# The side work of a three-layer sequence model: attention by a table of steps, the order of the products beside it, and a scan in eleven steps

## The reference, cut to what matters

```
def _hybrid_mixer(u, w_in, ...):
    proj = jnp.einsum('bsd,dp->bsp', u, w_in).astype(f32)
    (mq, mk, mv, mo, mi, mf, rq, rk, rv, rg, gq, gk, gv, gz, ga, gb) = jnp.split(proj, offsets, axis=-1)
    h_m = _mlstm(_heads(mq, M_HEADS), _heads(mk, M_HEADS), _heads(mv, M_HEADS), i_pre, f_pre)
    y_m = _head_rmsnorm(h_m, m_out_norm) * jax.nn.sigmoid(mo)
    h_r = _retention(_rope(_heads(rq, R_HEADS)), _rope(_heads(rk, R_HEADS)), _heads(rv, R_HEADS))
    y_r = _head_rmsnorm(h_r, r_out_norm) * jax.nn.silu(rg)
    qkv = jax.nn.silu(_causal_dwconv(jnp.concatenate([gq, gk, gv], axis=-1), g_conv))
    cq, ck, cv = jnp.split(qkv, 3, axis=-1)
    h_g = _gated_delta(_l2norm(_heads(cq, G_HEADS)), _l2norm(_heads(ck, G_HEADS)), _heads(cv, G_HEADS), ...)
    y_g = _head_rmsnorm(h_g, g_out_norm) * jax.nn.silu(gz)
    return jnp.einsum('bsm,md->bsd', jnp.concatenate([y_m, y_r, y_g], axis=-1).astype(u.dtype), w_out)
```

## Time and profile before

| | |
|---|---|
| median of three runs | 3654.03 us (3653.55 to 3658.63) |
| profiled execution | 3651.84 us, its span 3650.0 us, granted clock 0.967 |
| PE busy | 3389.2 us, 93% of the span |
| DVE, ACT busy | 1726.5 us (47%), 1334.7 us (37%) |
| attention, layer 0 | 436.0 to 625.2 us |
| delta rows, layer 0 | 625.2 to 709.4 us |
| attention and delta rows, layer 1 | 1628.0 to 1897.0 us |
| from the last Mamba products through LRU | 2893 to 3266 us |

### The profile page before, as it was taken

How to read it: one execution, slowest core, us unless ns; L and a number is a source line. 1 busy time by engine, 2 the same in 40 slices (tenths; PEclk the granted TensorE clock), 3 DMA queues, 4 the chain that set the end, 5 groups by cost and what they waited for, 6 DMA issues and landing times.

```text
span 3650.0 us, 38903 instructions
## 1 busy us (share of the span) xinstructions
PE 3389.2 (93%) x15366; PEld 2733.5 (75%) x15366; DVE 1726.5 (47%) x2415; ACT 1334.7 (37%) x1892; POOL 30.4 (1%) x62
## 2 busy tenths in 40 slices
PE   8999987799999999998878999998998988899998
PEld 6888755587888888876558788877777776678887
DVE  4443444655443444344465544455544556454433
ACT  4332334333332333233433333345444446433322
POOL 0000000000000000000000000000000000000000
PEclk9999999899999999999989999999999999999999
DMA  4333211103333233331110333321211222233232
GB/s 138 98 96 95 88 53 58 32 25 100 97 96 96 93 98 95 96 93 52 58 31 25 98 98 96 95 75 48 68 52 47 85 82 67 74 106 98 94 96 66
DMA packets 107396, 288.05 MB, mean 79 GB/s; under 512 B 22912, under 2 KB 34176, under 8 KB 107216
## 3 DMA queue, kind: packets, MB, share of 16 engines
q1 hardware_dynamic: 91696, 278.70, 24.6%
q10 hardware_dynamic: 14208, 2.63, 0.4%
q0 software_dynamic: 1312, 4.25, 0.4%
HBM read 282.64 MB, written 2.88 MB: 78 GB/s over the span
## 4 chain that ended last, share of the span: by engine, by line
PE 76%; DVE 11%; ACT 9%; issue 3%; DMA 1%; ACTq 0%; DVEq 0%; SPq 0%
PE ps L703 23%; PE ps L705 22%; PE ps L704 22%; DVE wl L1839 3%; ACT wh L1295 3%; DVE mf L2021 2%; PE ps L712 2%; PE ps L1024 1%; PE ps L1019 1%; DVE mf L2031 1%; PE ps L1190 1%; PE ps L717 1%; PE ps L1172 0%; PE ps L1186 0%; ACT mf L1427 0%
## 5 line engine op out<-in xcount | busy, mean ns | idle before, releaser
L1839 DVE TENSOR_TENSOR wl<-raw,wh 128x1024 fp32r<-128x1024 f32 (+3 forms) x581 | 651.8, 1123 | 1447.2 <-ACT wh L1295 1445.3
L703 PE MATMUL ps<-hnh,wh 128*128 128x512 f32 x2712 | 1098.6, 405 | 57.6 <-DVE mf L2516 29.0
L704 PE MATMUL ps<-hnl,wh 128*128 128x512 f32 x2712 | 1070.3, 395 | 0.0
L705 PE MATMUL ps<-hnh,wl 128*128 128x512 f32 x2712 | 1069.0, 394 | 0.0
L1295 ACT ACTIVATE wh<-raw 128x1024 fp32r<-128x1024 f32 (+3 forms) x581 | 567.1, 976 | 1046.7 <-PE ps L705 1027.9
L703 PEld LDWEIGHTS ps<-hnh,wh 128*128 128x128 f32 x2712 | 520.3, 192 | 201.2 <-issue 37.2
L705 PEld LDWEIGHTS ps<-hnh,wl 128*128 128x128 f32 x2712 | 517.7, 191 | 111.7
L704 PEld LDWEIGHTS ps<-hnl,wh 128*128 128x128 f32 x2712 | 519.5, 192 | 108.7 <-issue 4.3
L703 PE MATMUL ps<-mr,wh 128*128 128x512 f32 x1300 | 512.8, 394 | 16.4 <-DVE h L1965 9.3
L704 PE MATMUL ps<-mr,wh 128*128 128x512 f32 x1300 | 508.2, 391 | 0.0
L705 PE MATMUL ps<-mr,wl 128*128 128x512 f32 x1300 | 508.2, 391 | 0.0
(11 more groups left out here) (324 smaller groups left out, 2554.2 us busy)
## 6 DMA issues: line engine op xcount, KB each, us to landing
raw<-in_w_in SPq DMA_DIRECT2D x140, 512.0 KB, 3.5
raw<-in_ffn_w_gate SPq DMA_DIRECT2D x88, 512.0 KB, 3.5
raw<-in_ffn_w_up SPq DMA_DIRECT2D x88, 512.0 KB, 3.5
raw<-in_ffn_w_down SPq DMA_DIRECT2D x64, 512.0 KB, 3.5
raw<-in_w_ffn_in SPq DMA_DIRECT2D x44, 512.0 KB, 3.5
raw<-in_ffn_w_down SPq DMA_DIRECT2D x32, 384.0 KB, 3.1
raw<-in_w_out SPq DMA_DIRECT2D x32, 256.0 KB, 2.7
raw<-in_w_out_ssm SPq DMA_DIRECT2D x32, 256.0 KB, 2.6
```

What stands on the lines that cost most here:

```text
L703: self.e.matmul(out, ah, bh, start=start, stop=False, skip_group_check=shared)
L704: self.e.matmul(out, ah, bl, start=False, stop=False, skip_group_check=shared)
L705: m = self.e.matmul(out, al, bh, start=False, stop=stop, skip_group_check=shared)
L1839: self.e.tensor_tensor(lo[:, 0:n], k.raw[u % NRAW][:, 0:n], hi[:, 0:n].bitcast(F), ALU.subtract).then_inc(k.w_lo, 1)
```

## The change

**Attention.** The generator becomes a table of 65 steps. Step t does for head `t // 8` what its phase `t % 8` says, and beside it the norm of the pair before. All four scores of a head are issued at once into four banks (6, 7, 2, 3); spread and norm sums get a bank of their own (4). Rope starts at step 34, retention at step 40 with four steps a head. The four gated multiplies are put behind the table, since they need the gates, and the delta rows on ACT wait for the last of them. Zeroing and table loads on POOL start earlier.

**Order and pace.** The products beside the attention are now retention's q, k, v, the eight delta products, and gates 0 to 3 last. The paces rise.

**LRU.** The scan is cut into eleven steps, one operation for both channels each; the branch products 4 to 7 stand within the loop and behind it; gate product 8+i is followed by output product i at once. Of the rewritten functions only the new lines stand here.

```
 
-PACE_ROWS, PACE_ATT, PACE_DELTA = 0.9, 0.8, 1.0
-PACE_SSM_ROWS, PACE_SSM, PACE_LRU, PACE_LRU_GATES = 1.1, (1.1, 0.82, 0.82, 0.9), 0.25, 0.4
+PACE_ROWS, PACE_ATT, PACE_DELTA = 1.1, 0.98, 1.3
...
+ATT_STEPS, AT_ROPE, AT_RET = 65, 34, 40
+
...
         self.delta_qkv(l, 1)
-        self.qk_done = True
+        self.gates(l, y, 0, ACT.Sigmoid)
+        self.gates(l, y, 2, ACT.Silu)
         self.until(*self.work)
         self.pace = PACE_DELTA
         heads = [self.delta(l, h, y) for h in range(4)]
...
+        for t in range(ATT_STEPS):
+            h, s = divmod(t, 8)
+            p = h // 2 - 1
+            self.mlstm(l, h, s)
+            if 0 <= p < 2:
+                self.mlstm_pair(l, p, t - 16 * p - 16)
+            self.rope(l, t - AT_ROPE)
+            if t >= AT_RET:
+                h, s = divmod(t - AT_RET, 4)
+                self.retention(l, h, s)
+                for p in range(2):
+                    self.retention_pair(l, p, t - AT_RET - 8 * p)
+            yield
+        while len(self.gates_done) < 4:
+            yield
+        self.gated(l, y)
...
+        if s == 0:
+            self.wait_ge(k.row_v, 5 * l + 2)
+            self.wait_ge(*k.rows_v.at(l, "acol"))
+            if h:
+                self.wait_ge(*V.at(n - 1, "w3"))
+            if h == 3:
+                self.wait_ge(*k.mp_v.at(2 * l, "sum"))
+            self.spread(k.slot(M_NG, dt=R), h, B_PAIR, P.up(n, "sp"))
+            self.wait_ge(k.took, self.qk_took[2 * l])
+            for jt in range(4):
+                self.score(M_Q, M_K, h, jt, P.up(n, f"s{jt}"))
+        if s == 6:
+            self.wait_ge(k.took, self.v_took[2 * l])
+            if h:
+                self.wait_ge(*A.at(n - 1, "abs"))
+            for jt in range(2):
+                self.wait_ge(*V.at(n, f"w{jt}"))
+                self.values(M_V, M_D, h, jt)
+        if s == 7:
+            self.wait_ge(*V.at(n, "w2"))
+            self.values(M_V, M_D, h, 2)
+            self.wait_ge(*V.at(n, "w3"))
+            self.values(M_V, M_D, h, 3).then_inc(*P.up(n, "v"))
...
+        if s == 2:
             self.wait_ge(k.row_v, 5 * l + 1)
+            self.wait_ge(*k.mh_v.at(4 * l + min(2 * p + 2, 3), "dm"))
+            self.e.matmul(k.ps[B_PAIR][:, :], k.selr[0:64, 32 + 128 * p:160 + 128 * p], k.slot(M_EM, dt=R)[0:64, :],
+                          start=True, stop=True).then_inc(*k.mp_p.up(n, "pair"))
+        if s == 5:
+            self.wait_ge(*k.mp_a.at(n, "sq"))
+            self.e.matmul(k.ps[B_PAIR][:, :], k.c("bd64"), k.slot(M_Y + p)[:, :], start=True, stop=True).then_inc(*k.mp_p.up(n, "nm"))
...
+        if s == 0:
+            self.wait_ge(*(V.at(n - 1, "w3") if h else k.rope_v.at(4 * l + 3, "x")))
+            for jt in range(4):
+                self.score(R_Q, R_K, h, jt, P.up(n, f"s{jt}"))
+        if s == 3:
+            self.wait_ge(k.took, self.v_took[2 * l + 1])
+            self.wait_ge(*(A.at(n - 1, "num") if h else k.mh_a.at(4 * l + 3, "abs")))
+            for jt in range(4):
+                self.wait_ge(*V.at(n, f"w{jt}"))
+                m = self.values(R_V, R_D, h, jt)
+            m.then_inc(*P.up(n, "v"))
...
+        self.wait_ge(*k.att_v.at(l, "y3"))
...
+        if i < 2:
+            self.wait_ge(*self.k.mp_p.at(2 * l + i, "nm"))
         self.e.tensor_tensor(y[:, :], self.bank()[:, :], self.k.rs[:, :], ALU.mult).then_inc(self.k.took, 1)
 
...
+        for p in range(5):
+            u = [k.slot(L_U[p % 2] + i) for i in range(2)]
+            yl = [k.slot(L_YL[p % 2] + i) for i in range(2)]
+            for i in range(2):
+                self.product_h()
+                self.end_taps()
+                self.taps = self.lru_conv(p, i, u[i])
+            for i in range(2):
+                self.product_h()
+                self.take_yl(p, i, yl[i])
+                if i == 0:
                     self.end_taps()
+                    for j in range(2):
+                        self.split_u(p, j, u[j], uh[j])
+            if p in (1, 3):
+                self.branch_acc(4 + p // 2)
             self.finish()
+            self.lru_gates(p, uh)
+            self.uh_unit = self.u
+            self.work.append(self.scans(p, y))
+        self.pace = PACE_LRU_END
+        self.branch_acc(6)
+        self.branch_acc(7)
+        gate = [k.slot(n) for n in L_GATE]
+        parts = [k.pair(L_UH + i, L_LO[i]) for i in range(8)]
         for i in range(8):
+            self.product_h()
+            if i == 0:
+                self.gate_acc(7)
+            self.take_branch(8 + i, gate[i % 2], 8 + i)
+            self.finish()
             self.product(y, lambda j: (k.scan_a.at(j // 2, f"hi{j % 2}"), k.scan_v.at(j // 2, f"lo{j % 2}")))
+            self.take_mix(i, gate[i % 2], parts[i])
...
+        for t in range(SCAN_STEPS):
+            for i in range(2):
+                if t == 1:
+                    self.wait_ge(*V.at(p, f"la{i}"))
+                    e.activation(th[i][:, :], r[i][:, :], ACT.Tanh).then_inc(*A.up(p, f"tanh{i}"))
+                if t == 2:
+                    e.activation(r[i][:, :], r[i][:, :], ACT.Exp, scale=-1.0).then_inc(*A.up(p, f"a{i}"))
+                if t == 3:
+                    self.wait_ge(*A.at(p, f"a{i}"))
+                    e.activation(sq[i][:, :], r[i][:, :], ACT.Square).then_inc(*A.up(p, f"a2{i}"))
+                if t == 5:
+                    self.wait_ge(*V.at(p, f"t{i}"))
+                    e.activation(th[i][:, :], th[i][:, :], ACT.Sqrt).then_inc(*A.up(p, f"root{i}"))
+                if t == 9:
+                    self.wait_ge(*V.at(p, f"y{i}"))
+                    e.activation(y[2 * p + i][0][:, :], u[i][:, :], ACT.Copy).then_inc(*A.up(p, f"hi{i}"))
             yield
...
-            if h >= 2:
+            if h < 2:
+                e.wait_ge(*(k.mh_p.at(4 * l + 3, "sp"), k.mp_p.at(2 * l + 1, "pair"))[h])
+            else:
                 e.wait_ge(*k.rh_v.at(4 * l + h - 2, "w3"))
             e.dma_start(k.slot(R_TAB[h % 2])[:, :], k.I["ret"][h]).then_inc(k.loaded[f"ret{h % 2}"], 16)
-        e.wait_ge(*k.rp_v.at(2 * l + 1, "y"))
+            if h == 1:
+                e.wait_ge(*k.mh_p.at(4 * l + 3, "v"))
+                e.memset(k.slot(D_T1, dt=R)[:, :].bitcast(F), 0.0).then_inc(k.zeroed, 1)
+                e.memset(k.slot(D_T2, dt=R)[0:64, :].bitcast(F), 0.0).then_inc(k.zeroed, 1)
```

More of the change, by code:

```diff
@@ L485, in attention, with gated @@
     def attention(self, l, y):
-        yield
-        yield
-        yield from self.mlstm(l, y)
-        yield from self.rope(l)
-        yield from self.retention(l, y)
+        for t in range(ATT_STEPS):
[14 more added lines that the diff above has]
+        self.gated(l, y)
+    def gated(self, l, y):
+        pass
     def prepare(self, l, heads):
@@ new lines, in rope @@
+    def rope(self, l, s):
+        k = self.k
+        if s == 0:
+            self.wait_ge(k.loaded["rope"], 16 * (l + 1))
+            self.wait_ge(*k.mh_v.at(4 * l + 3, "w3"))
+        if 0 <= s < 2:
+            for n in (2 * s, 2 * s + 1):
+                self.wait_ge(k.took, self.qk_took[2 * l + 1] - 3 + n)
+                self.e.matmul(k.ps[B_SCORE[n]][:, :], k.slot(R_D, 3)[:, 0:128], k.slot((R_Q, R_Q + 1, R_K, R_K + 1)[n])[:, :],
+                              start=True, stop=True).then_inc(*k.rope_p.up(4 * l + n, "rot"))
@@ L1274, in scans @@
     def scans(self, p, y):
-        yield
-        yield
-        yield
+        for _ in range(SCAN_STEPS):
+            yield
     def take_mix(self, i, gate, parts):
```

522 lines of the change are left out of this document (188 added, 334 removed).

## The result

The changed kernel takes **3611.8 us** (3610.0 to 3612.0), against 3655.5 us for the kernel before beside it: a ratio of 0.9879, 95% interval 0.9864 to 0.9895. It is faster by 43.7 us. The forecast was 3584 us, a gain of 70; the range, 3532 to 3634, holds the result. So the direction was right and about four tenths of the gain did not arrive. The question is which of the three terms was too large, and whether something else took time.

What follows compares the result with a forecast made beforehand. PE was taken to bound the kernel, so only vanished PE waits save time. Attention 33, delta rows 24 and LRU 12 sum to 69 us, giving 3584 us; the 8-in-10 range was 3532 to 3634.

Steps and rivals of the forecast that it cites:

- slower case: Rival: each convolution product beside attention holds its ring plus half a head's DVE and ACT work; 3684 us, chance 0.05.
- looser ring: Rival: DVE and ACT overlap better than walked, LRU gains 45 and attention 45 us; 3540 us, chance 0.22.
- LRU term: LRU: gain of 12 us, from products that now cover waits beside the scans; bounds 0 and 50.
- attention term: Attention of both layers: old PE waits go, smaller ones come; gains 19 and 14, together 33 us.
- three new waits that were walked: Attention, PE waits: pair matmul 2.0 us, head 3's values 6, second pair's norm sum 3.5.
- the clock loss follows the waits: 9.5 falls to 3.5: Attention of layer 0: with 13 us of waits against 23, low-clock loss falls from 9.5 to 3.5 us.
- seams: Attention of layer 0: cost of changes between product and small matmul, 0.2 to 0.4 us each, falls from 15 to 13.
- I take 4.6 and 2.8 us: Delta rows: waits for the rows' sums and beta rows fall from 7.9 and 6.2 us, 6.7 gained.
- what the pace moves behind the products: Delta rows: pace 1.3 puts 6.8 us of products among inversion and round-trip waits, gaining 5 to 6 a layer.
- The walk of the period: LRU: following DVE's and ACT's work in order gives a period of 34.0 us, practically the old 34.1.
- the cover: LRU: two of four periods take a fifth product of 5.4 us, become only 2 us longer; 6.8 us gained.
- The rule on table loads: ACT: the skill's 2.66 us a switch, not 1.28, would make the summed gain 58 us instead of 69.

Runs made afterwards that it cites:

- e9: e2 with squares of q no longer waiting for the last gated multiply, and remainder 0.0 at the third layer: 3598.1 us.
- e4: e2 with the pace of the delta rows at 1.0 again instead of 1.3: 3607.6 us.
- e2: Changed kernel with the remainder in `due` set to 0.80 at the third layer and 0 where each mixer begins: 3600.9 us.
- e5: e2 with LRU's scan put back into large pieces at the old pace of 0.25, branches and gates in new places: 3617.1 us.
- e1: Changed kernel with the remainder in `due` set to 0.80 instead of 0.48 where the third layer begins: 3601.4 us.

## Why the prediction was right or wrong

**Direction and range: right, with errors that partly cancel.** The attention's waits for its own multiplies went, the LRU stalls shrank, and neither the slower case nor the looser ring came (no LRU period is under 32.7 us). But 9 us of loss in Mamba and 15 too few in the delta rows stand beside an LRU term that was too small, and inside the attention term two errors cancel, as told below. One sign that I had named for the slower case was badly chosen: convolution evictions more than 8 us apart beside mLSTM. They are, with a mean of 10.8 us from the first to the last of these two:

```profile
497.57 0.68 DVE L2024 TENSOR_TENSOR mf<-ps,mf 128x512 f32<-128x512 f32 x1
...
573.08 0.68 DVE L2024 TENSOR_TENSOR mf<-ps,mf 128x512 f32<-128x512 f32 x1
```

But no wait of PE on such an eviction is left in this stretch; PE's own small matmuls and its waits for values and norms fill the distance. The sign had to be a wait of a product for L2024, not a distance. It was already exceeded before, where the eight evictions beside retention stand 10.0 us apart in the mean; the 6.65 us of the earlier trace rows are the shortest distance, at the stretch's end:

```profile
559.52 0.68 DVE L2031 TENSOR_TENSOR mf<-ps,mf 128x512 f32<-128x512 f32 x1
...
629.57 0.68 DVE L2031 TENSOR_TENSOR mf<-ps,mf 128x512 f32<-128x512 f32 x1
```

**Attention, 33 us forecast, 25.3 measured.** The three new waits that were walked came in size (2.0, 6, 3.5 us against 2.2, 6.6, 3.6). For the longest the path was only half right. The list on ACT ran 10 us as walked, to 508.59, but the head's weights on DVE then stood behind a whole convolution round as well, split, low part, eviction, tap and taps, and PE had more work of its own than the one product assumed:

```profile
509.64 1.23 DVE L1830 TENSOR_TENSOR wl<-raw,wh 128x1024 fp32r<-128x1024 f32 x1 [5.70 <-ACT wh L1289]
...
513.71 1.15 DVE L2263 TENSOR_TENSOR mf<-ps,mf 128x512 f32<-128x512 f32 x2
```

```profile
514.54 3.32 PE L1029 MATMUL ps<-mf,mf 128*128 128x512 f32 x4 [6.58 <-DVE mf L2263]
```

Two terms failed. I gave rope and the first values 1.5 us, and the trace has 0.3, 3.7 and 1.6, that is 4 us more in layer 0. And "the clock loss follows the waits: 9.5 falls to 3.5" did not come true:

```profile
436.30:609.30 173.00, 154.16 (x635) 113.16 (x633) 84.55 (x136) 68.76 (x80) 3.60 (x8) 0.95 0.19 61
```

At clock 0.95 over 173 us the loss, counted as in the forecast, is 8.7 us, nearly as it was. Eight waits, up to 6.6 us long, left the share of the low level, 1.2 GHz, as it was with fourteen of up to 4.8 us.

A third term hides this in the total. For layer 0 I had 10 us from waits, 6 from the clock and 2 from seams. The named waits gave some 4 (23 to 18.6) and the clock 1, and still the stretch went from 189.2 to 173.0. PE's idle time fell by 4.7 us only, its busy time by 11.5 (165.7 to 154.2, with 7 matmuls less in the window, about 1.6 us). What fell with it are the changes between product and small matmul: from 34 to 24 in either direction, counted over the same products in both traces. So the seams, which were given 2 us, are the largest part of this gain, by what is left over; no run was made for them alone.

**Delta rows, 24 us forecast, 9.0 measured in the changed kernel.** Both steps failed in size, here for layer 0. The first, "I take 4.6 and 2.8 us": 6.9 and 3.1 came, a gain of 4.1 and not 6.7. Four gate products between the convolutions and the squares help little when the Silu of the last gate and its table load stand on ACT right before them; e9 shows 2 us of it to be the new wait. The second, that what the pace moves behind the products is taken off the inversion and the round trip: the inversion fell from 6.4 to 1.0, but PE then had less left to do behind the store, and the wait for the round trip rose from 6.7 to 9.2, so the two gave 2.9 us and not 5 to 6. Small waits grew by 1.9 us besides. At pace 1.0 (e4) the beta rows wait 6.2 us as before the change, so their 3.1 is the pace's doing and not that of the gate products. In all the pace gave 3.6 and 4.7 us where the text had 5 to 6. In layer 1 the remainder of `due` took 5 us of this again (154.6 in the changed kernel, 149.7 in e2).

**LRU, 12 us forecast, 15.7 measured.** The walk of the period was right: 34.0 against 34.1 us without the fifth product, 36 against 35.6 and 37.9 with it, and the cover 6.8 against 6.6. The other 9 us, where the last scans had been given 5.5, no run takes apart. The text read from the walk that the cut itself gains nothing; e5 shows that in the new loop 13.8 us go with the cut and its pace. The walk compared the new period with the old kernel's, not with what the new arrangement would cost uncut, 36 and 40 us.

**Mamba, 0 forecast, +9.0 measured.** The sentence "cuts elsewhere I take at 0" failed. I had treated the paces as local. They are not: the remainder is carried into every later part. It could have been worked out before the run from the number of calls, as above.

**The rule on table loads.** The sum stood by the row and not by the page, and the row held: after a load of 1.28 us the next operation begins 0.01 us later in the changed order too, as this row of e2 and its successor show.

```profile
605.87 1.28 ACT L1574 ACT_TABLE_LOAD   x1
607.16 0.69 ACT L1574 ACTIVATE mf<-ps,col 128x512 f32<-128x512 f32 x1
```

The Trainium skill ("ScalarE: Activation LUTs", What ACT_TABLE_LOAD costs) counts 1.38 us of draining on top; with it the list before head 3's values would have been 5.5 us longer. The trace does not agree: in the changed kernel that list, from its first load at 499.11 us to the end of the exponential at 508.59, takes 9.5 us with its four loads of 1.28 us and no gap above 0.02.

**The sum.** By stretches: 25.3 + 9.0 + 15.7 - 9.0 = 41.0 us, and the span fell by 40.2, the medians by 43.7. With the remainder of the third layer set as before (e1) the change is worth 50.6 us by the span and 55.9 by the medians.

## What to carry to other kernels

A pace with a running remainder couples every part to all later ones: reset it where a part begins, or a change of pace in one place retunes another, here by 9 to 10 us. When two engines alternate on one chain, compute the period by walking both lists in order; here the walk met the mean period with the cut, 34.0 against 34.1 us, but said nothing on what the uncut step would cost in the new arrangement, 2.4 us a period, so walk that case too. When a forecast stretch comes near, check its terms: here the seams paid what waits and clock did not. And a wait that moves behind an engine's list has to be priced with all that stands in that list directly before it, table loads included.
